# Routing on sums that are not yet normalized, a top-k in two halves, and the prompt tile last

## What is computed

```
sh1, sc1, g1, sh2, sc2, g2 = adaln(cond, w_ada, b_ada)     # one set for sample, one for prompt
x = x + g1 * (y @ w_out)                                   # mixer's output projection, residual
h = rmsnorm(x, norm_ffn) * (1.0 + sc2) + sh2
aff = softmax(h @ w_router)                                # 16 experts
gate_vals, idx = top_k(aff^T, cap)                         # each expert picks 64 sample, 16 prompt tokens
hid = silu(xs @ w_gate) * (xs @ w_up);  out = hid @ w_down * gate_vals
x = x + g2 * scatter_add(out at idx)
y = rmsnorm(x, norm_final)
```

## Time and profile before

| | |
|---|---|
| median of 3 runs | 1139.35 us |
| profiled execution | 1137.44 us, span 1135.6 us |
| TensorE busy | 1005.3 us, 89% |
| VectorE, ScalarE, POOL busy | 336.7, 283.6, 85.2 us |
| mean granted TensorE clock | 0.947 |
| DMA | 279.27 MB, mean 246 GB/s |
| the chain that ended last | PE 78%, DMA 10%, issue 5%, DVE 4%, ACT 2% |

### The profile page before, as it was taken

The page is one execution under the profiler, slowest core; times in us unless marked ns, Lnnn a source line. Parts: engine busy times, 40 slices in busy tenths (PEclk is TensorE's granted clock), DMA queues, the critical chain, the costliest instruction groups (busy, mean ns, idle before and its releaser), DMA issues.

```text
span 1135.6 us, 17904 instructions
## 1 busy us (share of the span) xinstructions
PE 1005.3 (89%) x7893; PEld 470.0 (41%) x7893; DVE 336.7 (30%) x665; ACT 283.6 (25%) x430; POOL 85.2 (7%) x97
## 2 busy tenths in 40 slices
PE   2898899999999999956089999999999999999980
PEld 2554456666665664534033333333333333333330
DVE  2366546254353561332700201011020201102022
ACT  3228655354353651232000000010000001000002
POOL 3000000000000001000000010202010020201001
PEclk9999999989999999976579999999999999999995
DMA  9950013402207624134049999999999999999935
GB/s 315 387 211 18 1 31 128 151 3 80 80 12 274 247 107 192 74 113 183 2 145 385 364 397 409 388 410 393 405 401 396 408 390 409 392 405 401 396 134 199
DMA packets 82792, 279.27 MB, mean 246 GB/s; under 512 B 3809, under 2 KB 3970, under 8 KB 82754
## 3 DMA queue, kind: packets, MB, share of 16 engines
q1 hardware_dynamic: 74688, 253.24, 57.6%
q0 software_dynamic: 5680, 17.54, 5.5%
q10 hardware_dynamic: 2386, 7.94, 1.8%
HBM read 265.04 MB, written 13.67 MB: 245 GB/s over the span
## 4 chain that ended last, share of the span: by engine, by line
PE 78%; DMA 10%; issue 5%; DVE 4%; ACT 2%; SPq 0%; POOL 0%; ACTq 0%; DVEq 0%; POOLq 0%
PE pa L423 50%; PE p L423 23%; DMA ring<-in_w_up_dram 7%; DMA ring<-in_w_ada_dram 2%; PE p L817 1%; PE p L768 1%; DVE reg_e L1352 1%; ACT L873 1%; ACT reg_d L873 1%; DVE reg_a L1491 1%; PE p L702 1%; PE pa L771 0%; PE p L553 0%; PE pa L850 0%; ACT reg_b L873 0%
## 5 line engine op out<-in xcount | busy, mean ns | idle before, releaser
L423 PE MATMUL pa<-ring,reg_b 128*32 128x512 f32 (+1 forms) x3232 | 414.3, 597 | 1.9 <-DMA ring<-in_w_up_dram 1.1
L423 PEld LDWEIGHTS pa<-ring,reg_b 128*32 128x32 f32 (+1 forms) x3232 | 138.9, 115 | 260.2 <-issue 259.7
L423 PE MATMUL pa<-reg_a,ring 128*128 128x128 f32 (+1 forms) x832 | 235.1, 438 | 5.1 <-DVE reg_a L1164 5.1
L423 PE MATMUL p<-ring,reg_b 128*16 128x512 f32 x1536 | 174.1, 592 | 1.2
L423 PEld LDWEIGHTS pa<-reg_a,ring 128*128 128x128 f32 x832 | 127.5, 193 | 101.0 <-issue 101.0
L873 ACT ACTIVATE reg_b<-pa 128x512 f32<-128x512 f32 (+1 forms) x28 | 17.1, 612 | 324.9 <-PE pa L423 269.0
L1462 DVE TENSOR_TENSOR reg_b<-reg_b,pa 128x512 f32<-128x512 f32 x16 | 11.0, 687 | 279.2 <-PE pa L423 279.2
L423 PEld LDWEIGHTS p<-ring,reg_b 128*16 128x16 f32 x1536 | 47.2, 97 | 108.9 <-issue 108.9
L873 ACT ACT_TABLE_LOAD x67 | 86.0, 1283 | 8.1 <-issue 6.7
L873 ACT ACTIVATE reg_b<-p 128x512 f32<-128x512 f32 x24 | 14.3, 597 | 190.1 <-PE p L817 167.2
L873 ACT ACTIVATE reg_c<-reg_c 128x320 f32<-128x320 f32 (+1 forms) x86 | 43.4, 574 | 6.1 <-DVE reg_c L1274 4.7
(11 more groups left out here) (220 smaller groups left out, 694.0 us busy)
## 6 DMA issues: line engine op xcount, KB each, us to landing
ring<-in_w_gate_dram SPq DMA_DIRECT2D x32, 2048.0 KB, 15.2
ring<-in_w_up_dram SPq DMA_DIRECT2D x32, 2048.0 KB, 14.6
ring<-in_w_down_dram SPq DMA_DIRECT2D x32, 2048.0 KB, 15.5
ring<-in_w_ada_dram SPq DMA_DIRECT2D x12, 2048.0 KB, 9.1
ring<-in_w_in_dram SPq DMA_DIRECT2D x7, 2048.0 KB, 19.7
ring<-in_w_out_dram SPq DMA_DIRECT2D x2, 2048.0 KB, 16.1
reg_c<-mod_rows POOLq DMA_DIRECT2D x8, 512.0 KB, 9.1
sum_rows<-reg_a ACTq DMA_DIRECT2D x5, 512.0 KB, 4.3
```

Source lines behind the costliest of these rows:

```text
L423: return nc.tensor.matmul(out, lhsT, rhs, start=start, stop=stop, **kw)
```

## The change

- **Logits from unscaled sums.** The tile is turned as it stands in `acc` (`acc_turn`), right after the residual. The modulation scale goes into the router weights (`w_rs`, made by VectorE in unit 5), the shift into a bias of 16 numbers (`rt_bias`, sixteen 16-column products in unit 6), and the reciprocal root is applied to the logits in `softmax`. ScalarE writes the tile times its reciprocal root to `h_rows`, and the modulation is applied to the gathered rows, in the copies from PSUM: eight scaled copies for sample and eight for prompt rows in each pair.
- **Residual by halves** of 512 columns, with the squares by halves too.
- **Projections in short pieces between turns.** `y_sums(i, a, b)` takes a range of the sixteen k steps of a tile; turns, logits and affinity turns stand between the pieces.
- **Sample choice as two merged lists.** The best 64 of tiles 0 and 1 are found while the projections still run, the best 64 of tiles 2 and 3 after tile 3; the second list is read backwards and the larger of each pair is taken.
- **Prompt tile last.** Tile 4's residual and routing come after the sample list; the sample rows are gathered before the prompt's list is known; the prompt rows are turned inside the gate stage.

```diff
+                    for g in range(2):
+                        for k in range(KT):
+                            r = mm(p45[:, 768 + NE * g:768 + NE * (g + 1)], mods[:, 3 * KT + k, g:g + 1].to_broadcast([P, P]),
+                                   w_rt[:, k, :], k == 0, k == KT - 1)
+                    r.then_inc(rb_ps, 1)
...
-            def h_turn(i):
-                pe.wait_ge(h_ready, i + 1)
+            def acc_turn(i):
+                pe.wait_ge(acc_done, 2 * i + 2)
...
+            y_sums(2, 0, 4)
+            acc_turn(0)
+            y_sums(2, 4, 8)
             logits(0)
+            acc_turn(1)
+            y_sums(2, 8, 12)
             aff_turn(0)
             logits(1)
+            y_sums(2, 12, 16)
             aff_turn(1)
+            y_sums(3, 0, 2)
+            acc_turn(2)
+            y_sums(3, 2, 6)
             logits(2)
+            y_sums(3, 6, 10)
             aff_turn(2)
+            y_sums(3, 10, 16)
+            y_sums(4, 0, 2)
+            acc_turn(3)
+            y_sums(4, 2, 4)
             logits(3)
+            y_sums(4, 4, 6)
             aff_turn(3)
+            y_sums(4, 6, 16)
...
+            pe.wait_ge(topk_s, 1)
...
+            acc_turn(4)
             logits(4)
             aff_turn(4)
+            pe.wait_ge(topk_p, 1)
...
-                pe.wait_ge(xs_done, i * 2 + 2)
+                pe.wait_ge(xs_done, i + 1)
                 use("g", 0)
                 sample_sums("g", 0, 0, xsT, pa[0])
-                sample_sums("g", 0, 1, xsT, pa[0])
+                pe.wait_ge(g_p, i * 16 + 16)
+                sample_sums("g", 0, 1, xsT, pa[0], (0,))
+                turn_prompt_rows(i)
+                sample_sums("g", 0, 1, xsT, pa[0], (1, 2, 3))
+                pe.wait_ge(xp_done, i + 1)
                 prompt_sums("g", 0, rows_p, p45[:, 0:512])
...
+            for i in range(NT):
+                for half in range(2):
+                    act.wait_ge(acc_done, 2 * i + half + 1)
+                    r = A(dump[:, half * 512:half * 512 + 512], acc[:, i, half * 512:half * 512 + 512], ACT.Square, accum_out=ss_h[:, half, i:i + 1])
+                r.then_inc(ss2, 1)
                 act.dma_start(sum_rows[i * P:(i + 1) * P, :], acc[:, i, :]).then_inc(acc_store, 16)
                 act.wait_ge(h_sc, i + 1)
+                A(stat[:, 2, i:i + 1], stat[:, 1, i:i + 1], ACT.Sqrt, bias=eps[:, 0:1], scale=1.0 / D).then_inc(h_std, 1)
                 act.wait_ge(ht_ps, i + 1)
...
+                A(accT[i % 2], p45[:, :], ACT.Copy).then_inc(ht_done, 1)
                 act.wait_ge(mx_done, i + 1)
+                A(aff[:, i % 2, :], z_rt[:, i % 2, :], ACT.Exp, bias=sm[:, i % 2, 0:1],
                   accum_out=sm[:, i % 2, 1:2]).then_inc(ex_done, 1)
+                act.wait_ge(h_ready, i + 1)
...
+                chain(A(h_tok[i % 2], acc[:, i, :], ACT.Identity, scale=stat[:, 3, i:i + 1]))
+                act.dma_start(h_rows[i * P:(i + 1) * P, :], h_tok[i % 2]).then_inc(h_store[i % 2], 16)
...
+            residual(2, 0)
...
+            turned(1)
+            residual(2, 1)
+            best(half_row[0], val_h[0], idx_h[0], 0, 16)
+            norm_sum(2)
+            norm_rstd(2)
+            best(half_row[0], val_h[0], idx_h[0], 16, 40)
+            softmax(2)
+            best(half_row[0], val_h[0], idx_h[0], 40, 56)
+            turned(2)
+            residual(3, 0)
+            best(half_row[0], val_h[0], idx_h[0], 56, 64)
+            chain(V.tensor_copy(idf_h[0], idx_h[0]))
+            residual(3, 1)
+            norm_sum(3)
+            norm_rstd(3)
+            softmax(3)
+            turned(3)
+
+            best(half_row[1], val_h[1], idx_h[1], 0, CS)
+            back_idx, back_val = idx_h[1][:, ::-1], val_h[1][:, ::-1]
+            chain(V.tensor_copy(idf_h[1], back_idx))
+            chain(V.tensor_scalar(idf_h[1], idf_h[1], float(TS // 2), None, ALU.add))
+            chain(V.tensor_tensor(first, val_h[0], back_val, ALU.is_ge))
+            chain(V.tensor_tensor(val_s, val_h[0], back_val, ALU.max))
+            V.copy_predicated(idf_h[1], first, idf_h[0]).then_inc(topk_s, 1)
...
             def rows_in(count):
 
-                dve.wait_ge(xs_ps, count * 2 + 1)
-                V.tensor_copy(xsT.rearrange("p k n -> p (k n)"), p67[:, :]).then_inc(xs_done, 1)
-                dve.wait_ge(xs_ps, count * 2 + 2)
-                V.tensor_copy(xpT.rearrange("p k e n -> p (k e n)"), pa[0][:, 512:768]).then_inc(xs_done, 1)
+                dve.wait_ge(xs_ps, count + 1)
+                for k in range(KT):
+                    r = V.tensor_scalar(xsT[:, k, :], p67[:, k * P:(k + 1) * P], ffn_scale[:, k, 0:1], mods[:, 3 * KT + k, 0:1],
+                                        ALU.mult, ALU.add)
+                r.then_inc(xs_done, 1)
```

More of the change, by code:

```diff
@@ L192, in program @@
         out_p = reg_c[:, 3 * D:4 * D]
-        g2r = [reg_c[:, (4 + g) * D:(5 + g) * D] for g in range(2)]
-        def ps(name):
-            return ctx.enter_context(nc.psum_tensor(name, [P, 1024], F32))
-        pa = [ps("pa0"), ps("pa1")]
-        p45, p67 = ps("p45"), ps("p67")
         four = [pa[0], pa[1], p45, p67]
@@ L742, in _ @@
+            y_sums(4, 0, 2)
+            acc_turn(3)
+            y_sums(4, 2, 4)
             logits(3)
-            h_turn(4)
+            y_sums(4, 4, 6)
             aff_turn(3)
+            y_sums(4, 6, 16)
+            for half in range(2):
+                pe.wait_ge(y_ps, 2 * NT)
+                pe.sem_inc(freed[SLOT_OF[("out", half)][0]], 1)
+            pe.wait_ge(topk_s, 1)
+            pe.wait_ge(y_free, 2 * (NT - 1))
+            for m, src in enumerate((idf_h[1], val_s)):
+                for odd in range(2):
+                    mm(slots_in_s[64 * odd:64 * odd + 64, 8 * m:8 * m + 8], src, ident[0:NE, odd:NE:2])
@@ L745, in _ @@
+            mm(slots_in_s[0:CS, 16:24], idf_h[1], ident[0:NE, 1:NE:2]).then_inc(slots_ps, 1)
+            acc_turn(4)
             logits(4)
             aff_turn(4)
[L749 to L755 removed]
@@ L785, in use, with sample_sums @@
                         pe.wait_ge(loaded[s], i * 32 + 16 * (turn + 1))
-                def sample_sums(m, kh, half, xT, dst):
+                def sample_sums(m, kh, half, xT, dst, steps=(0, 1, 2, 3)):
                     cols = slice(half * 512, half * 512 + 512)
-                    for k4 in range(4):
+                    for k4 in steps:
                         k = 4 * kh + k4
@@ L1444, in _ @@
-            V.tensor_copy(row_p[:, 0:PAIRS], slot_p[:, :]).then_inc(slots_done, 1)
-            dve.wait_ge(g2_in, 32)
+            half_row = [affT[:, 256 * b:256 * b + 256] for b in range(2)]
+            for i in range(2):
+                for half in range(2):
+                    residual(i, half)
+            norm_sum(0)
+            norm_rstd(0)
+            softmax(0)
+            norm_sum(1)
+            norm_rstd(1)
+            turned(0)
+            softmax(1)
+            residual(2, 0)
@@ new lines, in _ @@
+            for g in range(2):
+                V.memset((idf_p[:, 0:16], idf_p[:, 32:48])[g], 0.0)
+            V.memset(row_s[:, :], 0)
+            V.memset(row_p[:, :], 0).then_inc(pads_done, 1)
+            turned(1)
[6 more added lines that the diff above has]
+            best(half_row[0], val_h[0], idx_h[0], 40, 56)
@@ new lines, in _ @@
+            V.tensor_copy(slot_s[:, :, :].rearrange("p a b -> p (a b)"), slots_in_s[:, 0:16])
+            norm_sum(4)
+            norm_rstd(4)
+            softmax(4)
+            turned(4)
+            best(affT[:, TS:T], val_p, idx_p, 0, CP)
+            chain(V.tensor_copy(idf_p[:, 16:32], idx_p))
+            V.tensor_scalar(idf_p[:, 16:32], idf_p[:, 16:32], float(TS), None, ALU.add).then_inc(topk_p, 1)
+            dve.wait_ge(slots_ps, 2)
+            V.tensor_copy(row_p[:, 0:PAIRS], slots_in_p[0:32, 0:8]).then_inc(rows_p_done, 1)
```

290 lines of the change are left out of this document (138 added, 152 removed).

## The result

The median went from 1138.42 us (1136.96 to 1140.55, four runs) to 1111.5 us (1108.45 to 1114.64, four runs). The ratio is 0.9748 with a 95% interval of 0.9712 to 0.9784. The forecast was 1103 with a range of 1095 to 1113. The profiled execution took 1108.55 us (span 1106.8) against the 1101.1 of the sum, so 7.5 us have to be found.

What follows compares the result with a forecast made beforehand. The prediction took TensorE, with idle holes mostly between 484 and 575 us, to bound the kernel. 1137.44 - 37.15 (start of the loop) + 0.8 (loop) gave 1101.1, or 1103 from the median; range 1095 to 1113.

Steps and rivals of the forecast that it cites:

- the 1101.1 of the sum: Whole kernel: the profiled execution of before, 1137.44 us, less 37.15 up to the loop, plus 0.8 in the loop.
- the rival of the low clock: Y sums: one low stretch of some 10 us delays the loop 3 to 5 us, two 8; 1106 to 1111; chance 0.22.
- The rival of a dearer round: Top-k on VectorE: a 256-column round costs nearly a 512-column one, 12.8 us in all; 1116; chance 0.06.
- The wait for the list: Tail: TensorE waits about 4.5 us instead of 21.4 for the sample list, which is ready at 517.5.
- the 20.0 us from list to loop: End of the tail: sample list ready at 517.5, then tile 4's chain and sample transposes, first loop product at 537.5.
- the rival of a load that holds ScalarE twice as long: ScalarE in the tail: a table load takes twice its 1.28 us, loop starts 4.5 us later; 1107; chance 0.01.
- the rival of the early load: ScalarE, every tile: exponential's table loaded before the copy of turned sums, 4.3 us later; 1107; chance 0.04.
- the loop loses what the tail wins: Expert loop: prompt rows' scaled copies stop TensorE in each of 8 pairs, kernel slower; 1140 or more; chance 0.02.
- the weight stream holds the end: Expert loop: no gain because the weight stream, DMA share 0.97, keeps the end where it was; 1139; chance 0.01.
- the term outside the tail: Unit 6, ahead of the y sums: bias sums add 3.6 us, so y sums start at 428.3 instead of 424.74.
- The 1107.7 in the paragraph on the table load: Tail: by the skill's 2.66 us table switch with 1.38 of drain, the loop starts 4.6 us later; not used.
- The cheaper one: Top-k on VectorE: a 256-column round at 1.07 us starts the loop 4 us earlier; 1099; chance 0.05.

Runs made afterwards that it cites:

- the repeated kernel: The changed kernel run once more with no edit, as the yardstick for the follow-up runs; median 1109.70 us, ratio 0.9727.
- the three others that have the edit: Modulation columns added before head states: in the changed kernel (1099.69 us), with bias by ones and copy ahead of root (1092.49), and those with waits filled (1084.79).

## Why the prediction was right, and where 7.5 us went

- **The forecast by its own signs: the range held, the point did not.** It was to be wrong if TensorE's clock is low between 468 and 504; it is, from 480 to 488. It named 66.2 us for a pair of the loop; 530.4 / 8 is 66.3. The median of 1111.5 lies just above the 1106 to 1111 of the rival of the low clock, but in the profile that rival's stretch costs only 1.7 us. Most of the miss (6.0 of 7.5 us) lies ahead of the y sums, for which the range had no term; that its upper end, made for other things, covered it is luck.
- **Where the time comes from: right.** The waits of 21.4 and 20.6 us went, as forecast, and the tail is 111.0 us where the schedule had 109.2. Undoing a part at a time puts prices on some of it: prompt tile last 7 to 10 us, two lists 5 in the schedule, short pieces 21.7 with VectorE's order left as it was. The turn of the unscaled sums and the residual by halves have no run of their own; for them speaks the wait for modulated rows that is gone.
- **Rounds over 256 columns: right.** MAX8 takes 0.41 us (about 0.4 forecast) and a round 1.47, on the line between the widths of the earlier trace rows. The rival of a dearer round is refuted.
- **The wait for the list: right**, 4.8 us against 4.5. It is ready at 525.6: the forecast's 517.5, the late start of 6.0, and 2.0 for the clock and small steps. The 2.0 us ahead of logits(1) and the 20.0 us from list to loop came out at 1.99 and 19.8.
- **Table load and root: right.** The root starts 1.29 us after the load. The drain of 1.38 us behind a load that the Trainium skill, "ScalarE: Activation LUTs", section "What ACT_TABLE_LOAD costs", describes is not seen here either, and the rival of a load that holds ScalarE twice as long falls with it. The exponential's table is loaded at 531.49, behind the copy of the turned sums, so the rival of the early load falls too.
- **Copies: mis-sized, and small.** Eight scaled copies take 2.64 us, not 2.3. One of 128x128 takes 0.404 us where I priced it by a 16x128 copy; they follow each other at 0.33.
- **Loop: right.** +0.9 us for +0.8. The scaled prompt copies stay covered, and the loop's DMA share is 0.97 as before. The rivals "the loop loses what the tail wins" and "the weight stream holds the end" are refuted.
- **The clock inside the y sums: the rival happened, at a third of its length.** The stretch from 480 to 488 has 0.79, that is 3.4 us at the low level, a cost of 1.7, where I had put 10 us and 3 to 5. In the repeated kernel it cost 3.4. Eight passes at 5.38 us show it, where 16 took 7.03 at the high clock. My reason for it, the 2.0 us gap, is not the whole cause: with a gap of 0.38 it stayed.
- **The step that failed is the term outside the tail, "I take 3.6 ... the y sums start at 428.3".** They started at 434.34. The 3.6 priced the bias products by their own duration (3.5 measured) and everything around them at the clock that the profile of before happened to have. Of the missing 6.0 us, 1.8 belong to the change (3.1 in the repeat): the low stretch behind its narrow passes, which came in all eight kernels that have them and in none without. The other 4.3 are a stretch in unit 5, one more in the units than before and the repeated kernel have; those have one alone, in unit 1. Such stretches vary between runs, and my sum, made against one execution, took them for a constant.
- **Slips in the working that decided nothing.** The 1107.7 in the paragraph on the table load is 4.6 over the forecast of 1103.0, not over the sum of 1101.1. The dearer round was charged for 16 rounds, though eight of them were to be covered; over eight it gives 6.4 us, not 12.8. The cheaper one gives 3.2, not 4. TensorE and the weight stream "within 1%" do not come out of the earlier trace rows, which have 526.7 of 529 and a share of 0.97.

What stays open: why the clock falls behind the 32 narrow passes although TensorE has no idle time there, and what the low stretch in the y sums needs: the kernels with the short pieces have one there with a wait of 2.0 us as with one of 0.38, and the one with long pieces has one behind a wait of 2.4 (498 to 501).

## What to carry to other kernels

Keep the bound engine supplied, and lay its order out as one with the engine that serves it: changing TensorE's pieces alone cost 21.7 us here, more than undoing the list or the tile order did. Price an inserted piece of narrow matrix work by what stands behind it as well, and look first whether one product can replace it: here 3.6 us of products cost 7 to 9. And read a saving of a few microseconds from several timings with their granted clocks, because where the low stretches of the profiled execution lie is partly chance.

## What the runs showed of the hardware

- The granted clock fell from the 2.4 GHz level to the 1.2 GHz level behind 32 passes of 128x16, although the changed kernel's trace has no wait of TensorE from 366 to 404 us: the projection behind them took 8.81 to 10.13 us in eight of eight kernels, 7.03 to 7.11 in the six without them.
- The clock also fell in units with waits of 1.55 us each, not only behind the 6.9 us gaps of the earlier trace rows. With these waits at 0.4 us, the clock of 180 to 376 us rose from 0.97 to 1.00 in the kernel before, and is 1.00, 1.00 and 0.99 in the three others that have the edit.
- Products that nothing reads, run while TensorE would wait, brought 7.7 us between medians for 16 of them, of which the first 40 passes of the loop show 2.5 (7.00 to 4.50 us).
- Of one program, timings from 1103.92 to 1115.71 us went with a mean granted clock from 0.963 to 0.951.
